# State-space forward slots: the projection unit stands between the carried output and the head products

## The reference, cut to what matters

```python
t = h @ w_in                                   # projection: gate z, and x, B, C
xbc = silu(dwconv(t[...]))                     # x (32 heads of 64), B, C (8 groups of 128)
# in chunks of L = 128 tokens, for each group of 4 heads, both directions:
decay  = exp(where(tri, a_cum[l] - a_cum[s], -inf))
y_diag = einsum((C @ B.T) * decay, x * dt)     # within the chunk
states = einsum(B, exp(a_cum[-1] - a_cum), x * dt)
h      = h * exp(a_cum[-1]) + states           # carried from chunk to chunk
y_off  = einsum(C, h_prev, exp(a_cum))         # from the carried state
y = (y_diag + y_off + x * d_skip) * silu(z)
y = y * rsqrt(mean(y * y over the group) + eps) * norm_g
```

## Time and profile before

| | before |
|---|---|
| median of 3 runs | 2699.55 us |
| lowest, highest | 2698.3, 2703.53 us |
| profiled execution | 2698.38 us |
| its span | 2696.6 us |
| PE busy | 2300.4 us (85%) |
| PEld busy | 1836.9 us (68%) |
| DVE busy | 1500.2 us (56%) |
| ACT busy | 1122.9 us (42%) |
| POOL busy | 606.8 us (23%) |
| mean granted clock of PE | 0.92 |

### The profile page before, as it was taken

How to read it: one execution, slowest core, us unless ns; L and a number is a source line. 1 busy time by engine, 2 the same in 40 slices (tenths; PEclk the granted TensorE clock), 3 DMA queues, 4 the chain that set the end, 5 groups by cost and what they waited for, 6 DMA issues and landing times. The chain is left out here.

```text
span 2696.6 us, 36389 instructions
## 1 busy us (share of the span) xinstructions
PE 2300.4 (85%) x12794; PEld 1836.9 (68%) x12794; DVE 1500.2 (56%) x3267; ACT 1122.9 (42%) x2838; POOL 606.8 (23%) x594
## 2 busy tenths in 40 slices
PE   6769989899898989989886799669999999998676
PEld 1328877777786777778664688557777777776455
DVE  1455685958778595867847422243454445444442
ACT  1314655536464553646444311233444444444321
POOL 0021434424343442434333000011111111110000
PEclk8879999899998989999887899879999999999688
DMA  7560001010100101010001633231112211220053
GB/s 257 175 186 34 24 17 55 16 41 23 40 24 17 55 17 42 21 40 24 28 9 35 218 102 94 88 86 46 43 47 63 63 40 48 63 62 26 8 175 98
DMA packets 117259, 172.05 MB, mean 64 GB/s; under 512 B 27576, under 2 KB 78008, under 8 KB 116824
## 3 DMA queue, kind: packets, MB, share of 16 engines
q1 hardware_dynamic: 117080, 169.73, 20.2%
HBM read 141.53 MB, written 30.13 MB: 64 GB/s over the span
## 5 line engine op out<-in xcount | busy, mean ns | idle before, releaser
L599 PE MATMUL sg_pP<-h_h_hi,sg_whi 128*128 128x512 f32 (+1 forms) x1152 | 445.2, 386 | 14.2 <-POOL sg_wlo L1039 14.2
L600 PE MATMUL sg_pP<-h_h_lo,sg_whi 128*128 128x512 f32 (+1 forms) x1152 | 423.7, 368 | 0.0
L601 PE MATMUL sg_pP<-h_h_hi,sg_wlo 128*128 128x512 f32 (+1 forms) x1152 | 423.2, 367 | 0.0
L599 PE MATMUL at_pP<-h_h_hi,at_whi 128*128 128x512 f32 (+1 forms) x640 | 254.5, 398 | 11.7 <-POOL at_wlo L1824 11.7
L599 PEld LDWEIGHTS sg_pP<-h_h_hi,sg_whi 128*128 128x128 f32 x1152 | 231.5, 201 | 47.0 <-POOL sg_wlo L1039 14.3
L600 PEld LDWEIGHTS sg_pP<-h_h_lo,sg_whi 128*128 128x128 f32 x1152 | 230.4, 200 | 32.5
L601 PEld LDWEIGHTS sg_pP<-h_h_hi,sg_wlo 128*128 128x128 f32 x1152 | 229.1, 199 | 34.0
L601 PE MATMUL at_pP<-h_h_hi,at_wlo 128*128 128x512 f32 (+1 forms) x640 | 238.8, 373 | 0.0
L600 PE MATMUL at_pP<-h_h_lo,at_whi 128*128 128x512 f32 (+1 forms) x640 | 237.8, 372 | 0.0
L1824 POOL TENSOR_TENSOR at_wlo<-at_wr,at_whi 128x1024 fp32r<-128x1024 f32 x32 | 76.1, 2379 | 599.3 <-ACT at_whi L1734 599.3
L919 ACT ACTIVATE sg_u<-sg_pP 128x512 f32<-128x512 f32 (+1 forms) x96 | 50.6, 527 | 334.3 <-PE sg_pP L601 334.3
(11 more groups left out here) (227 smaller groups left out, 5015.9 us busy)
## 6 DMA issues: line engine op xcount, KB each, us to landing
sg_wr<-in_w_ssd SPq DMA_DIRECT2D x48, 512.0 KB, 3.4
at_wr<-in_w_na SPq DMA_DIRECT2D x32, 512.0 KB, 3.5
at_bias<-bt SPq DMA_DIRECT2D x256, 64.0 KB, 2.2
op_yr<-y SPq DMA_DIRECT2D x10, 1024.0 KB, 7.5
md_mod_w<-in_ada_w SPq DMA_DIRECT2D x4, 2048.0 KB, 13.3
nt_mod_w<-in_ada_w SPq DMA_DIRECT2D x4, 2048.0 KB, 10.1
ts_mod_w<-in_ada_w SPq DMA_DIRECT2D x4, 2048.0 KB, 14.4
y<-sg_Z SPq DMA_DIRECT2D x16, 512.0 KB, 3.0
```

What stands on the lines that cost most here:

```text
L599: pe.matmul(out, w_hi[:, k, :], h_hi[:, k, t0:t0 + n], start=(k == 0), stop=False)
L600: pe.matmul(out, w_hi[:, k, :], h_lo[:, k, t0:t0 + n], start=False, stop=False)
L601: x = pe.matmul(out, w_lo[:, k, :], h_hi[:, k, t0:t0 + n], start=False, stop=(k == KT - 1))
```

## The change

In forward slots the tensor engine's `forth(g, c)` is cut in two. `forth_carried` has the carried output and the next decay arguments, `forth_inner` the head products and the state product. The unit, which came after both, now comes between them. Where a slot has no unit, the order is as it was. All instructions, their operands and their waits are the same, and no other engine's list is changed.

```diff
--- before.py
+++ after.py
@@ -810,10 +810,10 @@
                     pe.wait_ge(scF, g * (NCH - 1))
                 pe.matmul(pS[:, 0:UN], X[:, g % 2, B_, u0:u0 + P], xdb[:, :], start=True, stop=True).then_inc(stA, 1)
 
-            def forth(g, c):
+            def forth_carried(g, c):
+
                 n = g * NCH + c
                 u0 = ucol(c * P)
-
                 if c:
                     pe.wait_ge(scF, g * (NCH - 1) + c)
                 else:
@@ -828,6 +828,9 @@
                 if c + 1 < NCH:
                     args(g, c + 1)
 
+            def forth_inner(g, c):
+                n = g * NCH + c
+                u0 = ucol(c * P)
                 pe.wait_ge(mm_, n + 1)
                 pe.wait_ge(evA, (g + 1) * NCH)
                 if n:
@@ -891,9 +894,10 @@
                     if g and i < 2:
                         norms(g - 1, NCH + i)
                 for c in range(NCH):
-                    forth(g, c)
+                    forth_carried(g, c)
                     if units[g][NCH + c] is not None:
                         unit(units[g][NCH + c])
+                    forth_inner(g, c)
                     off_sum(g, c)
                     norms(g, c)
             norms(G - 1, NCH)
```

## The result

The changed kernel takes 2762.48 us (median of 4 runs, 2759.06 to 2763.91) against 2700.58 us (4 runs, 2698.3 to 2703.53) for the kernel before, run beside it: **a ratio of 1.0222, 95% interval 1.021 to 1.0234**. It is slower by 62 us. The forecast was 2742 us, with a range from 2688 to 2768. The span of the profiled execution grew from 2696.6 to 2761.6 us, by 65.0.

The account below looks back on a forecast made before the run. DVE with POOL was taken as the bound in slots with a narrow unit. Terms without the clock gave -0.2 us per group, clock dips 6.3: 6.1 times seven groups, +43, so 2742 us, range 2688 to 2768.

Parts of the forecast that it names:

- Full slots, plus 0.68: Slots 2, 5, 8 and the full-speed part of 4 and 7: the diagonal chain makes each 10.30 us instead of 9.62.
- The waits that vanish: Slot 1 loses its wait for POOL, 2.06 us; slots 4 and 7 lose 6.47 and 6.69, before the clock.
- Slots 3 and 6, plus 4.6 each: Slots 3 and 6: PE waits for late DVE and a diagonal held by POOL; 11.6 us instead of 6.99.
- rival 2: Slots 3 and 6: POOL does not hold the diagonal; 1.9 us per group, 2713 us; chance 0.10.
- Slot 9 and the clock: Slot 9 takes 6.8 us instead of 4.09; low clock costs 2.1 us at each dip.
- Rival 1: Forward slots: the clock stays up; -0.2 us per group, 2688 to 2702 us, likeliest 2698; chance 0.14.
- Rivals 3 and 4: 3: DVE and POOL separate in time, 2668 us, chance 0.11. 4: low clock over whole units, over 2768, chance 0.09.
- slots 0 and 1: Slot 0 waits some 0.4 us for the carried state, slot 1 about 0.7 for ACT's squares; together plus 1.1.
- three dips: Forward part: the clock falls three times per group instead of twice, 2.1 us each, 6.3 in all.

Follow-up runs that it names:

- e6: The changed kernel with the old order (all of `forth` ahead of the unit) in slot 8 alone: 2753.69 us, ratio 1.0184 to the kernel before.
- e4: The changed kernel with ten matmuls, product unused, added between sum and norm in slots 3 and 6 of groups 0 to 6: 2723.15 us, ratio 1.0096.
- e5: The changed kernel with the old order in slot 0 alone: 2727.70 us, ratio 1.0091 to the kernel before.
- e3: The kernel before with the new order in the narrow slots 0, 3 and 6 alone: 2749.98 us, ratio 1.0189.
- e1: The kernel before with the new order in slots 4 and 7 alone: 2668.35 us, ratio 0.9894.
- e2: The kernel before with the new order in the full slots 1, 2, 4, 5, 7 and 8: 2705.67 us, ratio 1.0023.
- e9: The changed kernel with each slot's norm products issued behind the next slot's carried output and decay arguments: 2716.00 us, ratio 1.0047 to the kernel before.
- e10: e1 with each slot's norm products issued one step later, as in e9: 2721.03 us, ratio 1.0063 to the kernel before.
- e7: The changed kernel with POOL making the low part for one eighth of a weight tile, from the fifth tile on: 2723.68 us, ratio 1.0072.
- e12: e1 with four matmuls, product unused, added between sum and norm in slots 4 and 7 of groups 0 to 6: 2667.29 us, ratio 0.9873.
- e8: The kernel before with POOL making the low part for one eighth of a weight tile, from the fifth tile on: 2635.43 us, ratio 0.975.

## Why the prediction came out as it did

*Full slots, plus 0.68.* Right for slots 5 and 8, with 10.21 and 10.25 us (10.30 forecast); in each L870 waits for the diagonal, the chain through the state product that the prediction laid out. The wait itself is 0.34 us where the prediction named 0.6 to 0.7. Slot 2, for which it named 10.3 as well, has 11.8; of that below.

*The waits that vanish.* Right. The one for POOL in slot 1 and those for the gated output in slots 4 and 7 are gone; slots 4 and 7 have 12.0 us (10.3 plus the clock's 2.1 forecast).

*Slots 3 and 6, plus 4.6 each.* Right in mechanism and size: 11.85 and 11.95 us against 11.6. The end of slot 3 of group 3 in the changed kernel:

```profile
840.81 0.71 PE L856 MATMUL sg_pY<-sg_ident,sg_yo 128*128 128x128 f32 x4 [1.06 <-DVE sg_yo L1221]
...
841.62 2.52 POOL L1043 TENSOR_TENSOR sg_wlo<-sg_wr,sg_whi 128x1024 fp32r<-128x1024 f32 x1
841.97 0.42 DVE L1233 TENSOR_TENSOR sg_hf<-sg_hf,sg_pS 128x256 f32<-128x256 f32 x1
842.31 1.92 DVE L1266 TENSOR_SCALAR sg_diag<-sg_ident,sg_rstd 128x128 f32<-128x128 f32 x1
...
844.28 0.49 PE L870 MATMUL sg_pT<-sg_diag,sg_ones 128*128 128x128 f32 x2 [2.76 <-DVE sg_diag L1266]
```

The sum waits 1.06 us (1.2 forecast). L1233, which reads PSUM, takes its usual 0.42 us in the middle of POOL's split; L1266, which reads SBUF, takes 1.92 instead of 0.28 and ends 0.1 us after the split. L870 then waits 2.76. The starts of L1233 in slots 2 and 3, 832.26 and 841.97, are 9.71 us apart, where the prediction had DVE's 9.72.

That decides rival 2. The Trainium skill (GPSIMD Engine Reference, Key points) speaks of contention for DVE instructions with two SBUF inputs or in a 2-port mode. L1266 has one SBUF tensor as input, so the first half of that rule would let it escape; the trace has it held for the rest of the split. The second half would hold it. Whether it ran in a 2-port mode no run here shows, so the trace does not speak against the page, only against the prediction's reading that the page gives rival 2.

*Slot 9 and the clock.* Slot 9 has 7.66 us, 3.6 more than before, and the stretch behind it 1.1 more: 4.7 together, where the prediction had 2.7 for the slot and 2.1 for its dip of the clock. e6 shows that both come from the new order in slot 8. The clock's share in slots 4 and 7 is shown by e4: with the idle time filled, 4.6 us per group go in slots 3, 4, 6 and 7; the prediction had 4.2 there. Rival 1, the clock stays up, fell.

*Rivals 3 and 4.* DVE did not fall apart in time from POOL: its step into slot 3 stayed at 9.7 us. The step from slot 3 to slot 4 grew, from 12.15 to 13.45 us in group 3 (14.1 in the mean of groups 1 to 6), because DVE waits for the state product there, so in slots 4 and 7 DVE is no longer the bound. The low clock reached less than 4 us into slots 4 and 7 and not over their whole units, and by e4 it cost 2.3 us each time (slots 3 and 4, or 6 and 7), not more than 2.8. Both rivals fell.

*The step that failed: slots 0 to 2.* The sum had -2.06 for slot 1, +0.68 for slot 2 and +1.1 for "slots 0 and 1", with L874 of slot 1 waiting "about 0.7 us (bounds 0 and 1.5)"; that is -0.3. Measured was +3.2: slot 0 +0.3, slot 1 +0.8, slot 2 +2.1. **The mechanism was named, the term was mis-sized.** L877 waited 1.79 us, above the upper bound; the sum waited 0.48 more; and the clock fell a fourth time in each group, at the end of slot 1 or the head of slot 2, which was not in the sum at all (three dips were forecast). Slots 3 to 8 came out 0.4 below the sum. So 3.5 too little per group in one place and 0.4 to 0.5 too much elsewhere make 3 us, seven times 21: the 20 us between 2742 and 2762. e5, after e3, shows that slot 0's new order is the whole of it: without it slots 0 to 2 take 25.8 us, 1.6 less than before, and 35 us go.

*What the edit adds up to.* Its parts, by the runs, each measured with other neighbours, so the sum is a rough one: in slots 4 and 7 alone it gains 31 us (e1). In all full slots it costs 7 us (e2), because slot 8's new order opens slot 9, and the diagonal chain adds 0.6 a slot. In slot 0 it costs 35 us (e5). What is left to the changed kernel from e2, by the table: slots 3 to 8 take 2.8 us more per group than in e2, which is the new order in slots 3 and 6, some 20 us. That makes 7 + 35 + 20, the 62 us measured.

*What stays open.* Whether slots 1 and 2 have a distribution that beats e1; whether the later norm, kept out of group 7, would be worth anything beside e1 (by the table, e9 would come to about 2702 without its 14 us there, still above e1); whether the head products alone behind the unit, with the state product left ahead of it, would cover the wait in slots 4 and 7 without making DVE wait elsewhere, since every kernel here moves the two together; and what fixes when the clock falls. These weren't tried.

## What to carry to other kernels

Before moving a long block of independent products on one engine, find out which engine sets the pace in each stage: here PE's wait of 3.7 us was only where DVE's lateness was paid, and moving the block moved the bill one slot earlier, with 0.6 us a slot and a clock dip on top. Put the block where it covers the wait and nowhere else; in the two slots of ten where PE stood for the gated output the same order gained 1.1%. Ask as well what the work that gets pushed behind the block feeds: here the state product did, and DVE stood 101 us for it. And look at what follows directly behind the product that another engine waits for: it is the thing that will wait next, and delaying it is only free if the engine that sets the pace does not wait for it in turn (e9 against e10).

## What the runs showed of the hardware

- **Two short waits can bring the clock down like a long one, and the length of one wait does not settle it.** In e7 the clock fell within the second of two waits of 1.06 and 1.12 us with a sum of 0.71 between them. A wait of 2.31 us was followed by 0.50. A wait of 2.06 us in slot 1 left it at 1.00 in the kernel before, but the same wait, 2.07 us, in slot 1 of group 2 of e1 was followed by 0.50, and that slot took 13.04 us instead of 11.44. Slot 4 of e2 took 12.2 us in some groups and 12.8 in others.
- **Filling idle time with matmuls that nobody reads paid 34 to 39 us** in one kernel (e4) and nothing in another (e12).
- **POOL's long instruction held a DVE instruction with a single SBUF tensor to its own end**: L1266 took 1.92 us instead of 0.28. L1188, with two SBUF tensors, took 2.45; L1227, also with two, takes 1.26 us beside POOL's low parts and 0.42 where POOL is idle (group 7 of the kernel before, starts 1454.49 and 1462.00), a better comparison than the prediction's, which took its 0.42 from L1229 with a PSUM input; L1233, with one input from PSUM, kept its 0.42 in the same stretch. Taking seven eighths of that POOL instruction away gave the kernel before 2.5% (e8), though POOL is busy only 23% of its span: no other single edit here was worth as much, and it is invisible in the share of busy time.
